# Per-tile waits at stage entries, and first-chunk weight splits moved to VectorE, in a hybrid attention layer on one core

## The reference, cut to what matters

```python
h = rmsnorm(x) * (1 + scale) + shift          # shift, scale, gate from silu(c) @ w_ada + b_ada
qa, ka, va, za, qb, kb, vb, zb, ga, gb = split(h @ w_in)
oa = neighbourhood_attention(qa, ka, va, cache_a)   # branch A, 8 heads of 64
ob = window_attention_with_sink(rope(qb), rope(kb), vb, cache_b)   # branch B, 8 query heads
ya = (oa * silu(za)) @ w_br_a
yb = (ob * silu(zb)) @ w_br_b
m  = sigmoid(ga) * ya + sigmoid(gb) * yb
y  = rmsnorm(x + gate * (m @ w_out)) * final_norm_g
```

## Time and profile before

| what | value |
|---|---|
| median of 3 runs | 1301.0 us (1300.32 to 1301.18) |
| the profiled execution, its own time | 1298.77 us |
| its span | 1296.9 us |
| PE busy | 1228.3 us, 95% of the span |
| DVE busy | 831.1 us, 64% |
| ACT busy | 617.6 us, 48% |
| POOL busy | 201.7 us, 16% |
| mean granted clock of PE | 0.99 |

### The profile page before, as it was taken

How to read it: one execution, slowest core, us unless ns; L and a number is a source line. 1 busy time by engine, 2 the same in 40 slices (tenths; PEclk the granted TensorE clock), 3 DMA queues, 4 the chain that set the end, 5 groups by cost and what they waited for, 6 DMA issues and landing times. The chain is left out here.

```text
span 1296.9 us, 23377 instructions
## 1 busy us (share of the span) xinstructions
PE 1228.3 (95%) x7888; PEld 1113.7 (86%) x7888; DVE 831.1 (64%) x1670; ACT 617.6 (48%) x1239; POOL 201.7 (16%) x207
## 2 busy tenths in 40 slices
PE   6999899999999999999899989999999997999997
PEld 1599788988998899899789989989988985988996
DVE  2469357846765775687488588588678874454352
ACT  3432225634543554355356456556546663543441
POOL 0000023103300520231000000000000036333430
PEclk9999999999999999999899999999999999999999
DMA  9346532133214213321511411321221556444440
GB/s 361 127 179 208 181 101 75 50 127 120 68 63 135 80 61 107 122 70 67 159 54 38 131 48 37 100 72 42 73 89 43 182 186 219 147 130 152 158 160 33
DMA packets 87257, 147.67 MB, mean 114 GB/s; under 512 B 7558, under 2 KB 65542, under 8 KB 87180
## 3 DMA queue, kind: packets, MB, share of 16 engines
q1 hardware_dynamic: 70476, 124.64, 29.7%
q10 hardware_dynamic: 16704, 22.15, 4.8%
HBM read 111.37 MB, written 35.40 MB: 113 GB/s over the span
## 5 line engine op out<-in xcount | busy, mean ns | idle before, releaser
L83 PE MATMUL d_ps_pairs<-h,wt 128*128 128x320 f32 x2304 | 359.3, 311 | 0.0
L83 PEld LDWEIGHTS d_ps_pairs<-h,wt 128*128 128x128 f32 x2304 | 338.8, 188 | 0.3
L1088 ACT ACTIVATE pr<-s_ps_pairs,mx 128x896 f32<-128x896 f32 (+1 forms) x160 | 142.9, 896 | 84.1 <-DVE mx L1316 43.5
L1273 DVE TENSOR_TENSOR pt<-t_ps_pairs,pt 128x512 fp32r<-128x512 f32 (+1 forms) x272 | 158.2, 620 | 37.3 <-ACT pt L1077 36.1
L83 PE MATMUL s_ps_pairs<-h,wt 128*128 128x512 f32 (+1 forms) x864 | 171.4, 360 | 7.5 <-DVE wt L1339 4.1
L83 PEld LDWEIGHTS s_ps_pairs<-h,wt 128*128 128x128 f32 x864 | 144.9, 194 | 30.2 <-DVE wt L1339 4.3
L1077 ACT ACTIVATE pt<-t_ps_pairs 128x512 fp32r<-128x512 f32 (+1 forms) x272 | 135.0, 546 | 36.2 <-PE t_ps_pairs L950 31.2
L950 PE MATMUL t_ps_pairs<-ident_sb,pr 128*128 128x128 f32 x960 | 133.0, 276 | 14.8 <-DVE pr L1332 7.1
L950 PEld LDWEIGHTS t_ps_pairs<-ident_sb,pr 128*128 128x128 f32 x960 | 108.3, 140 | 25.0 <-DVE pt L1273 13.5
L1720 PE MATMUL y_ps<-wo,mg 128*128 128x512 f32 x480 | 115.7, 401 | 8.1 <-POOL wo L1667 7.9
L1720 PEld LDWEIGHTS y_ps<-wo,mg 128*128 128x128 f32 x480 | 90.9, 191 | 31.2 <-issue 9.7
(11 more groups left out here) (169 smaller groups left out, 1693.1 us busy)
## 6 DMA issues: line engine op xcount, KB each, us to landing
gates_d<-gst ACTq DMA_DIRECT2D x96, 160.0 KB, 1.8
wraw<-in_w_gate SPq DMA_DIRECT2D x24, 512.0 KB, 3.4
gt<-gates_d SPq DMA_DIRECT2D x40, 256.0 KB, 4.0
comb_a<-in_bias SPq DMA_DIRECT2D x24, 384.0 KB, 3.3
vw_a<-v_d SPq DMA_DIRECT2D x64, 128.0 KB
v_d<-vst SPq DMA_DIRECT2D x20, 320.0 KB, 4.4
wada<-in_w_ada SPq DMA_DIRECT2D x12, 512.0 KB, 5.7
kk<-kb_d SPq DMA_DIRECT2D x16, 320.0 KB, 5.8
```

Of the source, the lines that this page charges most:

```text
L83: mm = eng.matmul(out, lhs(a, k), rhs(b, k), start=(k == 0 and i == 0), stop=(k == n_k - 1 and i == 2))
L1088: act.activation(probs_run(s, t), scores_run(s, t), ACT.Exp, bias=mx[:, t:t + 1], scale=-1.0, accum_out=den[:, t:t + 1]).then_inc(exp_done, 1)
L1273: dve.tensor_tensor(pt[:, 1, c * 512:c * 512 + cols], t_ps[:, n % 2, 0:cols], pt[:, 0, c * 512:c * 512 + cols].bitcast(F32), ALU.subtract) ...
```

## The change

It has three parts. The wait of PE for all tiles split ahead (L874) goes, in both branches; the waits of each projection and gate block stay. In `finish` all low parts of weight tiles are made by DVE, in the order of `EXTRA`, with one semaphore `w_lo`. In the first chunk PE's output projection goes through e, then k, then both halves n; both accumulations of an e then end together. The waits for `mg_lo` and for the tile are written for both e.

```diff
@@ pairs, block.tensor
-        pe.wait_ge(w_lo, BEFORE)
         def body(p, last):
@@
-DVE_TILES = [m for m in range(2, WT) if m < KD or m % 2 == 0]
-POOL_TILES = [m for m in range(2, WT) if m not in DVE_TILES]
@@ def wait_split(eng, f, m):
-    if m in DVE_TILES:
-        eng.wait_ge(f["w_lo_dve"], DVE_TILES.index(m) + 1)
-    elif m in POOL_TILES:
-        eng.wait_ge(f["w_lo_pool"], POOL_TILES.index(m) + 1)
+    if m >= 2:
+        eng.wait_ge(f["w_lo"], m - 1)
@@ finish, block.gpsimd
-        def lows(j):
-            for m in EXTRA[j]:
-                if m in POOL_TILES:
-                    pool.wait_ge(w_hi, m - 1)
-                    pool.tensor_tensor(weight(f, m, 1), weight_raw(f, m), weight(f, m, 0).bitcast(F32), ALU.subtract
-                                       ).then_inc(w_lo_pool, 1)
...
-                if first:
-                    lows(j)
@@ finish, block.tensor
+            def output(e, n, k):
+
+                for q, (a, b) in enumerate(((0, 0), (0, 1), (1, 0))):
+                    mm = pe.matmul(y_ps[:, e, n * 512:(n + 1) * 512], mg[:, a, k, e * P:(e + 1) * P],
+                                   wo[k][:, b, n * 512:(n + 1) * 512],
+                                   start=(k == 0 and q == 0), stop=(k == KD - 1 and q == 2))
+                if k == KD - 1:
+                    mm.then_inc(y_mm, 1)
+
             for e in range(2):
+                if first:
+                    for k in range(KD):
+                        pe.wait_ge(mg_lo, i * KD + k + 1)
+                        wait_split(pe, f, KD + k)
+                        for n in range(2):
+                            output(e, n, k)
+                    continue
                 for n in range(2):
-                    if not first:
-                        pe.wait_ge(gated, i * 4 + 2 * e + n - 3)
+                    pe.wait_ge(gated, i * 4 + 2 * e + n - 3)
                     for k in range(KD):
                         if e == 0 and n == 0:
                             pe.wait_ge(mg_lo, i * KD + k + 1)
-                            if first:
-                                wait_split(pe, f, KD + k)
...
+                        output(e, n, k)
@@ finish, block.vector
                 if first:
                     for m in EXTRA[j]:
-                        if m in DVE_TILES:
-                            tile_low_f(dve, f, m)
+                        tile_low_f(dve, f, m)
```

More of the change, by code:

```diff
@@ L1439, in tile_low_f @@
     dve.tensor_tensor(weight(f, m, 1), weight_raw(f, m), weight(f, m, 0).bitcast(F32), ALU.subtract
-                      ).then_inc(f["w_lo_dve"], 1)
+                      ).then_inc(f["w_lo"], 1)
 def first_silu(act, f, n):
@@ L1472, in finish_tables @@
     f["first_in"] = [sem(f"first_in{n}") for n in range(PIECES)]
-    for n in ("w_hi", "w_lo_dve", "w_lo_pool", "silu_done", "og_prod", "og_hi", "og_lo"):
+    for n in ("w_hi", "w_lo", "silu_done", "og_prod", "og_hi", "og_lo"):
         f[n] = sem(n)
@@ L1492, in finish @@
     b_ps, y_ps, wb, wo = f["b_ps"], f["y_ps"], f["wb"], f["wo"]
-    w_in, w_hi, w_lo_dve, w_lo_pool = f["w_in"], f["w_hi"], f["w_lo_dve"], f["w_lo_pool"]
+    w_in = f["w_in"]
     silu_done, og_prod, og_hi, og_lo = f["silu_done"], f["og_prod"], f["og_hi"], f["og_lo"]
```

## The result

The changed kernel takes 1281.85 us (median of 4 runs, 1279.62 to 1285.31), beside 1300.8 us for the kernel before in the same comparison (4 runs): a ratio of 0.9857 [0.9834, 0.9879]. Two later comparisons of the same pair gave 0.9879 [0.9861, 0.9897] and 0.9862 [0.9839, 0.9884]; the mean of the three is 0.9866, a gain of 17.4 us. The forecast was 14.2 us, 1286.8 us, and the range ended at 1283.8.

A forecast was written before the change was run, and what follows sets the result against it. PE, busy 95% of the span, was taken to bound the kernel. Entry A 4.4, entry B 6.1 and last stage 3.7 us sum to 14.2, from a median of 1301.0 to 1286.8 us; range 1283.8 to 1291.8.

The forecast's parts named there:

- the clock's share at entry A: Branch A's first projection: without the pause PE keeps full clock, giving back 1.1 us, at the least nothing.
- DVE's shift in the last stage: Last stage: tile 15's load moves 3.9 us earlier, and DVE's second-chunk first b_prod with it, 4.2 us in all.
- Entry of branch A: PE's first projection there: pause of 3.3 us goes and 1.1 us of clock returns, 4.4 us (3.0 to 4.4).
- Nothing is late: Branch A's first bias tile: brought forward 4.4 us, DVE still comes 1.0 us behind POOL, so no new wait.
- Entry of branch B: PE's first projection there: pause of 4.1 us goes and 2.0 us of clock returns, 6.1 us (3.8 to 6.1).
- The last stage: First to second chunk: DVE's shift of 4.2 us less 0.5 for low clock, 3.7 us (1.9 to 4.9).
- (a): Rival: the clock at the entries of both branches does not come back; gain 11.1 us, 1289.9 us; chance 0.09.
- (b): Rival: PE's new wait at the second chunk costs the low clock in full; gain 12.8 us, 1288.2 us; chance 0.10.
- (c): Rival: last stage keeps little, load 15 or its successors no earlier; shift 1 us, gain 11.5, 1289.5 us; chance 0.11.
- (e): Rival: the waits at the entries only change their name; gain 3.7 us, 1297.3 us; chance 0.03.
- (f): Rival: the change loses, the new wait dropping the clock throughout the second chunk; 1309.5 us; chance 0.02.
- (d): Rival: last stage, DVE's chain is shorter and PE's whole 10.7 us are had; gain 21.2, 1279.8 us; chance 0.06.

The follow-up runs named there:

- e1: Kernel before with only the two waits at the entries of branches A and B removed, last stage as before: ratio 0.9923 [0.9900, 0.9945].
- e5: The changed kernel timed again, unaltered, against the kernel before: ratio 0.9879 [0.9861, 0.9897].
- e2: The changed kernel with both entry waits put back, so only the last stage is changed: ratio 0.9963 [0.9949, 0.9978] to the kernel before.
- e16: Repeat of e2, only the last stage changed and both entry waits kept: ratio 0.9962 [0.9943, 0.9982] to the kernel before.
- e8: The changed kernel, with DVE emptying the first group of y_ps between the second and third oz piece in the first chunk: 1276.58 us, 0.9827 to the kernel before.
- e12: As e8, but the first chunk's output matmuls in the old order e, n, k: 1283.04 us, ratio 0.9872 [0.9849, 0.9895] to the kernel before.
- e6: Kernel before with only the wait at the entry of branch A removed: ratio 0.9971 [0.9960, 0.9982].
- e7: Kernel before with only the wait at the entry of branch B removed: ratio 0.9963 [0.9950, 0.9976].
- e15: Repeat of e1, both entry waits removed and the last stage as before: ratio 0.9905 [0.9883, 0.9926] to the kernel before.
- e14: The changed kernel timed a third time, unaltered, against the kernel before: ratio 0.9862 [0.9839, 0.9884].
- e4: Kernel before with only the order e, k, n of the first chunk's output matmuls; entry waits and POOL's low parts kept: ratio 0.9997 [0.9981, 1.0014].
- e13: Kernel before with only the early emptying of y_ps in the first chunk, as in e8: ratio 0.9991 [0.9979, 1.0004].
- e3: Kernel before with all low parts on DVE; entry waits and the old order of output matmuls kept: ratio 0.9973 [0.9959, 0.9987].

## Why the prediction was wrong, step by step

The measured gain was larger than forecast. Where the time would come from was right. Two terms of the sum were too small, the clock's share at entry A (1.1 us, measured 1.7) and DVE's shift in the last stage (4.2 us, measured 5.5), the range had almost no room above its terms, and the offset of 2.2 us between profiled execution and median was only 0.4 after the change.

**Entry of branch A: 4.4 forecast, 5.1 found.** The pause of 3.34 us went whole. The clock term was mis-sized: 1.1 us, and it is 29.43 - 27.75 = 1.7. I had worked out the time at full clock from the paces of the last stage as 28.2 us and taken that for exact, with nothing above it in the range; the changed kernel does the same 144 matmuls in 27.75.

**"Nothing is late" in branch A: false.** POOL, DVE and PE after the change, at the first bias tile, against the earlier trace rows; then PE's pause there in the kernel before, and in e1:

```profile
185.02 1.88 POOL L866 TENSOR_TENSOR comb_a<-comb_a,colm_a 128x384 f32<-128x384 f32 x1
...
186.94 1.23 DVE L1284 TENSOR_REDUCE mn<-s_ps_pairs 128x2 f32<-128x1024 f32 x1 [0.91 <-POOL comb_a L866]
...
190.65 0.73 PE L977 MATMUL o_ps_pairs<-pt,vp_a 128*128 128x256 f32 x4 [1.91 <-DVE pt L1272]
```

```profile
195.32 0.74 PE L978 MATMUL o_ps_pairs<-pt,vp_a 128*128 128x256 f32 x4 [0.55 <-DVE pt L1273]
```

```profile
191.69 0.73 PE L977 MATMUL o_ps_pairs<-pt,vp_a 128*128 128x256 f32 x4 [2.52 <-DVE pt L1272]
```

POOL begins its bias tiles at the same time as before (182.21 against 182.44), because their load sets it, and one instruction took 1.88 us where it took 1.02. So the slack of 1.0 us was used up, DVE waits 0.91 us, and PE's pause there grew from 0.55 to 1.91. This is no accident of one execution: the pause is 0.53 to 0.55 us in the 7 profiled executions with the wait at entry A, and 1.80 to 2.52 us in the 9 without it. In two of these 9, e1 and e5, a low clock follows it, which costs about 1.6 us more. Against it, PE's pause of 1.03 us on DVE's `pr`, at 184.55 us before, is gone in the changed kernel, so the net loss is smaller.

The 1.2 us by which the rest of branch A got shorter is scatter of this pair, and 0 was the right forecast. From the first scores to the end of the branch it takes 441.4 to 445.4 us in the 7 executions with the entry wait (mean 443.6) and 442.2 to 445.4 in the 9 without it (mean 444.0). PE's small waits in it sum to 8.8 to 12.0 us with the entry wait and to 9.4 to 11.7 without.

**Entry of branch B: 6.1 forecast, 6.3 found.** Pause and clock as read. The sign "begins near 617.4" came out as 615.3, by the 0.7 us more at entry A and the scatter of 1.2 us in the rest of branch A.

**The last stage: 3.7 forecast, 4.7 found in the pair, 4.8 and 4.9 by the times of e2 and e16.** The mechanism was right in each link: the load of tile 15, the `oz` pieces, DVE, the new wait of PE of about 4 us (3.80) in place of its stall, and a gain that is DVE's and not the 10.7 us. The mis-sized term is DVE's shift: 5.5 us and not 4.2; over the five executions with this stage it is 5.2 to 6.9. Of the 1.3 us too little, 0.7 was there already at the load of tile 15 (4.6 against 3.9), and most of the rest is the 0.76 us by which DVE's first operation on the fourth piece got shorter (1.57 to 0.81). In the kernel before it was:

```profile
1098.76 1.57 DVE L1732 TENSOR_TENSOR oz<-oz 128x512 f32<-128x512 f32 x1 [0.35 <-ACT oz L1615]
```

The prediction would lay this to POOL's long low parts of weight tiles, but the last of those had ended at 1087.6. What ran beside the operation was POOL's low part of the third `oz` piece (1098.49 to 1099.78); after the change it runs from 1080.40 to 1081.69 and the operation starts only at 1081.42. That the overlap made it slow fits both rows, and no run took it apart.

Against it the low clock behind the new wait, with the second wait, cost 19.71 - 17.44 = 2.3 us where 1.4 + 0.5 = 1.9 were forecast. From the third block to the second chunk's output matmuls the five executions lose 1.5 to 2.7 us. e5, where the clock stays up, loses 1.5 with the second wait alone, and e2 and e16, where it falls, lose no more: there the low clock costs nothing beyond the second wait, which is the prediction's argument for a small price. The order over k at nothing was right for this change, and e8 with e12 shows where it would not be.

**The sum and the range.** In the profiled pair the three terms give 5.1 + 6.3 + 4.7 = 16.1 us, and the scatter in the two branches 1.1 more, 17.2 in all against 14.2. The forecast median missed by 4.95 us. Some 3.1 of this is what the profiled execution gained beyond the forecast. The other 1.9 arose because the forecast put the median 2.2 us above the profiled execution, as it was before, while after the change it lay 0.4 above; that part is scatter. The means over the profiled executions, with the old and with the new code of each stretch, are a firmer measure than the one pair: entry A 5.2 us, entry B 6.2, and the last stage 84.0 us (before, e1, e6, e7, e15) against 77.8 (the first execution of the changed kernel, e2, e5, e14, e16), 6.2, which lies inside the intervals of e2 and e16. Together that is 17.6, beside 17.4 by the three comparisons. Each term had erred to the same side, and the ends allowed 0 us above the entry terms and 1.2 above the last stage: 15.4 us at the most, and 1.8 more for scatter brought the low end to 1283.8. That was the mistake of the range: "at full clock it takes" was itself an estimate, from other stages, and deserved an end above it.

**The rivals.** (a) is out. What the prediction held for it was misread: the 75 matmuls of 19.34 us stand right behind the pause of 3.21 us, not in a stretch without pauses, and the windows of the kernel before show 0.50 from 1088 to 1091 us. The busy time by window after the change, where the earlier trace rows had 0.50:

```profile
150.00:152.00 2.00, 2.00 (x10) 1.65 (x10) 0.62 (x1) 0.49 (x1) 1.44 (x2) 1.00 0.56 67
...
619.00:621.00 2.00, 2.00 (x11) 1.64 (x10) 1.50 (x6) 1.66 (x4) 0.00 (x0) 1.00 1.12 390
```

(b), by which the new wait costs a low stretch of its own, has the low stretch right in four of five executions and the price half right in the first. (c) and (e) are out by e2, e16, e1 and e15; (f) by the steady chunks, where PE still has no gap and the clock is back from 1099 us on. (d) gave 1279.8 us, near the measured time, but for a reason that did not occur: PE's stall was not had, as the 3.80 us show. A time near a rival's is not evidence for it.

## What to carry to other kernels

When a stall is taken from the engine that bounds the kernel, ask which other engine arrives next and follow its chain: that chain's shift is the gain, and the difference comes back as a new wait. Then look inside that chain for work whose order is free, since edits that are worth nothing alone (the order over k in e4, the early emptying in e13) can be worth 5 us together; test them in pairs before dropping them. Leave an open end on the side of gain too, above all where a term rests on a pace that was measured in another stage. And before explaining a difference of 1 us in one pair of profiles, look at the same stretch in every profile at hand: here it was scatter.

## What the runs showed of the hardware that I had not expected

**Every pause at the entries was followed by the lower clock, and none without.** Of 16 profiled executions, the 7 with the pause of 3.3 to 3.4 us at entry A show a low granted clock behind it and the 9 without it don't; at entry B, 4.1 to 4.8 us, it is 7 and 9 again. At the new wait it is less plain. The busy time by window (length, busy time of PE, PEld, DVE, ACT and POOL, granted clock, DMA share, GB/s) in the first execution of the changed kernel, then in e5:

```profile
1089.00:1091.00 2.00, 0.49 (x5) 0.28 (x3) 1.97 (x3) 1.99 (x3) 0.00 (x0) 1.00 0.00 0
1091.00:1093.00 2.00, 0.00 (x0) 0.00 (x0) 1.97 (x4) 0.26 (x2) 0.00 (x0) 0.61 0.65 262
1093.00:1095.00 2.00, 1.70 (x8) 1.70 (x9) 0.58 (x2) 1.98 (x3) 0.74 (x1) 0.50 0.00 0
1095.00:1097.00 2.00, 2.00 (x11) 2.00 (x11) 1.23 (x2) 1.97 (x4) 0.92 (x1) 0.50 0.00 0
1097.00:1099.00 2.00, 2.00 (x14) 2.00 (x13) 1.66 (x5) 1.20 (x3) 1.55 (x2) 0.69 0.46 178
```

```profile
1091.00:1093.00 2.00, 0.00 (x0) 0.00 (x0) 1.97 (x4) 0.26 (x2) 0.00 (x0) 1.00 0.65 262
1093.00:1095.00 2.00, 1.72 (x14) 1.73 (x15) 0.55 (x2) 1.98 (x3) 0.73 (x1) 1.00 0.00 0
1095.00:1097.00 2.00, 1.41 (x12) 1.20 (x11) 1.25 (x2) 1.97 (x4) 0.93 (x1) 1.00 0.00 0
```

In the first the clock falls to the lower level, 1.2 GHz, while PE stands, and comes back some 5 us after it works again. In e5 the wait was 2.42 us long and a second one of 1.18 followed, with 1.00 throughout. But e16 with 2.61 us of wait shows the fall, its 144 matmuls taking 18.96 us. The Trainium skill (TensorE: Matmul & The Clock Gate, "Why this matters for your kernels") asks to avoid idle gaps of PE between bursts of matmuls above a certain length, since the clock then goes back to half rate. The pauses at the entries are above the length that it names, and they agree. The waits of e5 and e16 are below it, so e5 does not speak against the page; e16 shows that staying below it is no assurance.

**Shorter pauses can do it as well.** In e3, in the third turn of branch A, which the edit does not touch, PE stood for 1.22 and 0.46 us, and the windows that follow show a low clock:

```profile
432.00:434.00 2.00, 1.54 (x6) 1.30 (x6) 1.47 (x4) 1.97 (x5) 0.00 (x0) 0.70 0.73 256
434.00:436.00 2.00, 2.00 (x8) 1.71 (x7) 1.33 (x2) 0.14 (x1) 1.88 (x2) 0.50 0.00 0
```

The kernel before has pauses of 0.97 and 0.46 us at the same place with 1.00 throughout. This place comes in the second to fourth turn of all 16 profiled executions, 48 times. The pause was 1.19 to 1.33 us in 14 of them, and 6 of these were followed by a low clock; it was 1.01 us or less in the other 34, and none of these was. Why 8 of the 14 were not, no run shows. A stretch as at entry A costs 1.7 us. Between executions of one kernel such stretches come and go, and longer executions tend to have the lower mean clock: the four of the first comparison of the changed kernel have spans of 1277.8, 1279.7, 1280.4 and 1283.5 us at 0.996, 0.993, 0.994 and 0.991. It is not the whole of the scatter, as `front` alone differs by 2 to 3 us between profiled executions. A gain of a few us is to be judged by the stage's own length in several profiles and by repeated comparisons, not by one pair.
